# A reordered opening, input powers in two halves of the pairs, and half of the power turns ahead of the inner matrices, in a two-layer hybrid encoder

## The chip, the cores and the metric

The kernel runs on 1 core of one Trainium2 chip. The metric is the device time of one execution in microseconds (us); the median over runs is quoted. PE is TensorE, DVE is VectorE, ACT is ScalarE, POOL is GpSimd, SP is SyncE (here only a DMA queue).

## The reference, cut to what matters

Two pre-norm layers over 256 tokens of 1024 channels, and a final norm. A layer normalizes, projects with `w_in` (1024 x 4096) to q, k, v, the input u of a state-space mixer and four blocks of gate logits, and merges differential attention and the mixer:

```
xn = rms_norm(x, norm_mix[layer]); proj = xn @ w_in[layer]
q, k = rotary(q), rotary(k);  a = diff_attention(q, k, v, lam)
# s5_bidirectional, per direction, 32 groups, 64 complex states:
b_bar = ((a_bar - 1.0) / lam)[..., None] * b_mat
states = associative_scan(a_bar, einsum(b_bar, u));  y = y + real(einsum(c_mat, states))
s = gelu(y); s = s * sigmoid(s @ w_glu)
x = x + (gates0 * (a @ w_branch0) + gates1 * (s @ w_branch1)) @ w_out
x = x + (swiglu in layer 0, top-2-of-8 expert swiglu in layer 1)
```

## The kernel before, in words

Every engine has its own program, written out by hand, and semaphores order them. A weight tile is 128 x 2048 float32 (1 MB) in one of 3 (later 11) `raw` buffers. Each product is made of three: ACT copies the tile to a rounded `hi`, DVE subtracts to get `lo`, and PE multiplies hi by hi, lo by hi and hi by lo, 24 matmuls of 512 columns for a tile. `split_static(t)` is ACT's and DVE's share of tile t, `split_half(t, half)` the same in two halves, `proj` PE's. SP loads tile t once `lo` of tile t-3 is made. Two tiles are one block of 512 output columns: tiles 0 and 1 are u, 2 and 3 v, 4 and 5 q, 6 and 7 k (into the PSUM banks `PJ`), and tiles 8 to 15 (gates) are spread over the eight steps of the score loop.

The mixer works in chunks of four tokens, so it needs powers of the state factor times the input matrix. In layer 0 DVE makes them: `next_factor(k)` makes the small factors, `input_power(whole(bbar), 0)` the matrix itself, `input_power(b_power(k), k)` the powers 1 to 4, each over all 16 pairs of groups: four operations of 512 elements a partition, then two subtractions and two additions that lay the result out. In layer 1 POOL makes them long ahead. PE then transposes the powers in eight turns (`b` turns, one for each two pairs; ACT copies each to SBUF; the turns alternate between the two banks `TR`), and multiplies the small inner matrices of the chunks (`inner(l)`: 256 matmuls of 64 columns and 16 with the diagonal `kdiag`). `b_part` and `b_ready` tell PE that the powers are made.

After the inner matrices ACT copies them in two parts (`inner_copies`), and 16 DMAs of SP (`inner_moves`, `cbm_in`) lay them out; the first use is `y_inner` in step 0 of the score loop, right behind tile 8. Step s of that loop: PE scores(s), transposed weights, one weight tile, inner outputs, `s5_out(s)`; DVE `row_max`, `lo` of a tile, `softmax_factors`, `rotated(s+1)`, `weights(s)`, `scanned(s+1)`; POOL turns the scanned states back (`turn_forward`), for which `s5_out` waits.

PE's order around the change is: tiles 0 to 3, u transposes, tiles 4 to 7, q transposes, `inner`, k transposes, eight b turns with the first state matmuls between them, scores. POOL makes the parameters (`par_ready`) from two sines of ACT.

## Time and profile before

| what | value |
|---|---|
| runs of the kernel before | 1391.1, 1395.47, 1395.57 us; median 1395.47 |
| the profiled execution | 1390.18 us, of which the span is 1388.4 us |
| PE busy | 1350.3 us, 97% |
| DVE busy | 1107.1 us, 80% |
| ACT busy | 897.8 us, 65% |
| POOL busy | 332.5 us, 24% |
| chain that ended last | PE 86%, DVE 6%, ACT 3% |

The chain is the work followed back from the last instruction. A busy PE is counted from modelled ends. Times in the rows are from the start of the span, so the 1.8 us between the time and the span lie outside of them.

### The profile page before, as it was taken

How to read it: one execution, taken by the hardware profiler on the slowest of the kernel's cores; microseconds unless marked ns; L12 is line 12 of the kernel's file. 1: busy time of each engine (PE TensorE's matmuls, PEld its weight loads, DVE VectorE, ACT ScalarE, POOL GpSimd, SP SyncE). 2: the span in 40 equal slices, each digit the busy share in tenths (PEclk: the TensorE clock that was granted, in tenths of full speed). 3: DMA queues.
4: the chain of work that ended last, by engine and by line, in shares of the span. 5: the costliest groups of instructions: out<-in, count | busy, mean ns of one | idle time of the engine just before them, and what ended most of it. 6: DMA issues, size and time to landing. Idle time of an engine off the chain costs nothing.

```text
span 1388.4 us, 22394 instructions
## 1 busy us (share of the span) xinstructions
PE 1350.3 (97%) x7982; PEld 1108.9 (80%) x7982; DVE 1107.1 (80%) x1013; ACT 897.8 (65%) x915; POOL 332.5 (24%) x425
## 2 busy tenths in 40 slices
PE   8889999999999999999999999999999999999996
PEld 6678787888888787878888888888888888888885
DVE  6988678555565686788888889888888888898886
ACT  6366745444454566457777777777777777777775
POOL 7958419994000384010000000000000000000100
PEclk9999999999999999999999999999999999999998
DMA  8342355655645432979999999999999999999991
GB/s 330 122 127 104 137 171 193 197 182 186 198 145 173 132 123 99 351 264 339 369 374 377 386 366 377 391 362 387 379 375 388 368 375 390 352 391 350 386 347 31
DMA packets 194574, 385.12 MB, mean 277 GB/s; under 512 B 17616, under 2 KB 56912, under 8 KB 194384
## 3 DMA queue, kind: packets, MB, share of 16 engines
q1 hardware_dynamic: 189392, 369.99, 74.0%
q0 software_dynamic: 3360, 12.06, 2.9%
q10 hardware_dynamic: 1760, 2.23, 0.5%
q8 instruction: 39, 0.64, 0.2%
q14 instruction: 23, 0.19, 0.0%
HBM read 375.85 MB, written 7.34 MB: 276 GB/s over the span
## 4 chain that ended last, share of the span: by engine, by line
PE 86%; DVE 6%; ACT 3%; issue 2%; DMA 1%; SPq 1%; POOL 1%; ACTq 0%; POOLq 0%; DVEq 0%
PE bank L698 80%; DVE lo L1747 3%; ACT hi L1303 1%; PE bank L1197 1%; PE bank L716 1%; PE bank L842 1%; DMA raw<-in_w_in_dram 1%; PE bank L867 1%; PE bank L954 0%; PE bank L1180 0%; POOL raw L2346 0%; PE bank L1071 0%; ACT raw L1353 0%; ACT at_hi L1654 0%; PE bank L824 0%
## 5 line engine op out<-in xcount | busy, mean ns | idle before, releaser
L1747 DVE TENSOR_TENSOR lo<-raw,hi 128x2048 fp32r<-128x2048 f32 x344 | 801.7, 2342 | 153.7 <-ACT hi L1303 153.0
L1303 ACT ACTIVATE hi<-raw 128x2048 fp32r<-128x2048 f32 x344 | 658.0, 1916 | 186.3 <-PE bank L698 183.6
L698 PE MATMUL bank<-hi,at_hi 128*128 128x512 f32 x1288 | 513.5, 399 | 14.3 <-DVE lo L1747 3.4
L698 PE MATMUL bank<-hi,at_lo 128*128 128x512 f32 x1288 | 503.6, 391 | 0.0
L698 PE MATMUL bank<-lo,at_hi 128*128 128x512 f32 x1288 | 502.8, 391 | 0.1
L698 PEld LDWEIGHTS bank<-hi,at_hi 128*128 128x128 f32 x1288 | 242.7, 188 | 68.6 <-issue 7.6
L698 PEld LDWEIGHTS bank<-hi,at_lo 128*128 128x128 f32 x1288 | 242.5, 188 | 52.3
L698 PEld LDWEIGHTS bank<-lo,at_hi 128*128 128x128 f32 x1288 | 242.8, 189 | 47.9 <-DVE lo L1762 0.5
L698 PE MATMUL bank<-hi,ht_hi 128*128 128x512 f32 x432 | 168.8, 391 | 0.9 <-DVE ht_lo L2212 0.9
L698 PE MATMUL bank<-hi,ht_lo 128*128 128x512 f32 x432 | 168.2, 389 | 0.0
L698 PE MATMUL bank<-lo,ht_hi 128*128 128x512 f32 x432 | 168.1, 389 | 0.0
L2435 POOL TENSOR_TENSOR small<-cst 128x1 f32<-128x1 f32 x14 | 5.9, 422 | 591.0 <-DVE slot_row L2249 298.7
L698 PEld LDWEIGHTS bank<-hi,ht_hi 128*128 128x128 f32 x432 | 81.1, 188 | 19.2 <-DVE lo L1747 1.5
L698 PEld LDWEIGHTS bank<-hi,ht_lo 128*128 128x128 f32 x432 | 81.1, 188 | 17.0
L698 PEld LDWEIGHTS bank<-lo,ht_hi 128*128 128x128 f32 x432 | 81.2, 188 | 16.6
L1663 ACT ACTIVATE ht_hi<-bank 128x512 fp32r<-128x512 f32 (+1 forms) x48 | 26.9, 561 | 55.8 <-PE bank L1197 55.8
L1659 ACT ACTIVATE vreg<-bank 128x512 f32<-128x512 f32 (+1 forms) x48 | 27.1, 565 | 25.1 <-PE bank L698 25.1
L2341 POOL MEMSET raw<- 128x4 f32 x4 | 0.3, 105 | 156.4 <-DVE raw L1850 156.4
L1327 ACT ACTIVATE at_hi<-bank 128x512 fp32r<-128x512 f32 x28 | 15.4, 596 | 32.6 <-PE bank L716 32.6
L2212 DVE TENSOR_TENSOR ht_lo<-bank,ht_hi 128x512 fp32r<-128x512 f32 (+1 forms) x48 | 30.7, 640 | 1.7 <-ACT ht_hi L1663 1.7
L1608 ACT ACTIVATE ht_hi<-bank 128x512 fp32r<-128x512 f32 x10 | 6.0, 599 | 38.9 <-PE bank L1071 38.9
L2208 DVE TENSOR_TENSOR vreg<-vreg,bank 128x512 f32<-128x512 f32 (+1 forms) x48 | 30.5, 636 | 0.0
(312 smaller groups left out, 1172.5 us busy)
## 6 DMA issues: line engine op xcount, KB each, us to landing
raw<-in_moe_w_dram SPq DMA_DIRECT2D x528, 512.0 KB, 6.7
raw<-in_ffn_w_dram SPq DMA_DIRECT2D x66, 512.0 KB, 4.4
raw<-in_w_in_dram SPq DMA_DIRECT2D x64, 512.0 KB, 4.6
raw<-in_w_branch_dram SPq DMA_DIRECT2D x16, 512.0 KB, 4.4
raw<-in_w_out_dram SPq DMA_DIRECT2D x16, 512.0 KB, 4.8
raw<-in_w_glu_dram SPq DMA_DIRECT2D x4, 512.0 KB, 4.3
moe_sum<-xres POOLq DMA_DIRECT2D x3, 512.0 KB, 6.0
qk<-in_x_cols_dram SPq DMA_DIRECT2D x2, 512.0 KB, 6.2
```

The source lines that it names most:

```text
L698: return pe.matmul(o, a, b, start=start, stop=stop)
L716: last = pe.transpose(bank[:, i * rows:(i + 1) * rows], src, ident[0:rows, 0:rows])
L842: last = pe.matmul(o[rows, :], cblk[rows, r, q, 4 * d:4 * d + 4, :].rearrange("p i h -> p (i h)"), states, start=False, stop=m % 4 == 3 an ...
L867: m = pe.matmul(bank[r0:r0 + GC, c0:c0 + 64], bbar[rows, r, q, d, :], cblk[rows, r, q, 4 * d:4 * d + 4, :].rearrange("p i h -> p (i h)"), ...
L1197: m = pe.transpose(TR[0][:, f * P:(f + 1) * P], v_flat[:, f * P:(f + 1) * P], ident)
L1303: act.activation(hi[:, slot, :], src, ACT.Copy).then_inc(hi_ready, 1)
L1327: act.activation(at_hi[:, k0:k0 + kn, c0:c0 + P], bank[:, 0:kn * P].rearrange("p (k c) -> p k c", k=kn), ACT.Copy, scale=scale).then_inc(a ...
L1659: act.activation(v_flat[:, 0:h_width(c)], PJ[0][:, 0:h_width(c)], ACT.Silu).then_inc(g_ready, 1)
L1663: act.activation(ht_rows_hi[:, 0:h_width(c) // P, :], TR[0][:, 0:h_width(c)].rearrange("p (f s) -> p f s", s=P), ACT.Copy).then_inc(ht_hi_ ...
L1747: tt(lo[:, slot, :], src, hi[:, slot, :].bitcast(f32), SUB).then_inc(lo_ready, 1)
L2208: tt(v_flat[:, 0:h_width(c)], v_flat[:, 0:h_width(c)], right, MUL).then_inc(h_done, 1)
L2212: tt(ht_rows_lo[:, 0:h_width(c) // P, :], TR[0][:, 0:h_width(c)].rearrange("p (f s) -> p f s", s=P), ht_rows_hi[:, 0:h_width(c) // P, :].b ...
```

## The change

It does nine things. (1) x's second half of columns is loaded ahead of the token rows `xres`, and the loads of constants and parameters are spread behind tiles 3 to 6; (2) all of tiles 0 to 3 are split and multiplied in halves, and v (tiles 2, 3) goes to the banks `TR`; (3) ACT makes six of x's eight gained parts (before, four) and DVE two, and ACT's sines and squares stand behind the halves of tiles 1 and 2; (4) tiles 4 and 5 (q) go ahead of the u transposes on PE; (5) DVE makes the input powers in two halves of the pairs, pairs 8 to 15 of all powers first, after q's rotation; (6) the b turns 6, 7, 4, 5 go ahead of `inner` and the k turns, in both layers; (7) the diagonal `kdiag` is loaded ready-made; (8) the attention lambdas are summed after k's rotation; (9) in the score loop DVE does `rotated`, `softmax_factors`, `scanned`, `weights`, and `lo` last.

```diff
-B_TURNS = (6, 7, 0, 1, 2, 3, 4, 5)
+B_EARLY, B_LATE = (6, 7, 4, 5), (0, 1, 2, 3)
...
                         if t == 1:
-                            sp.dma_start(xres[:, :, :].rearrange("p t d -> p (t d)"), x_rows).then_inc(x_in, 16)
                             sp.dma_start(x_flat[:, 1024:2048], x_cols[:, 1024:2048]).then_inc(cols_second, 16)
                         if t == 3:
-                            sp.dma_start(cst[:, C_ID:C_ID + P], consts[:, C_ID:C_ID + P]).then_inc(ident_in, 16)
+                            sp.dma_start(xres[:, :, :].rearrange("p t d -> p (t d)"), x_rows).then_inc(x_in, 16)
+                        if t == 4:
                             sp.dma_start(braw_flat, ssm_b[0, :, :]).then_inc(b_in[0], 16)
+                        if t == 5:
...
                 pe.wait_ge(rot_ready, 4 * l + 2)
                 for th in range(TH):
                     transposes((l, "q", th), heads_of(qk[:, 0, :, :], th))
-                inner(l)
-                pe.wait_ge(rot_ready, 4 * l + 4)
-                for th in range(TH):
-                    transposes((l, "k", th), heads_of(qk[:, 1, :, :], th))
-                pe.wait_ge(b_ready, l + 1)
-                for g in B_TURNS:
+                pe.wait_ge(b_early, l + 1)
+                for g in B_EARLY:
+                    power_turn(g)
+                inner(l)
+                pe.wait_ge(rot_ready, 4 * l + 4)
+                for th in range(TH):
+                    transposes((l, "k", th), heads_of(qk[:, 1, :, :], th))
+                pe.wait_ge(b_ready, l + 1)
+                for g in B_LATE:
+                    power_turn(g)
...
+                    x_hi((0, 1))
+                    split_half(0, 0)
+                    split_half(0, 1)
                     act.wait_ge(lr_ready, 1)
                     act.activation(row(R_er), row(R_lr), ACT.Exp)
+                    act.wait_ge(cols_second, 16)
+                    x_hi(range(4, KD))
+                    split_half(1, 0)
+                    split_half(1, 1)
                     act.wait_ge(angle_ready, 1)
                     act.activation(par[:, SIN, :], row(R_red), ACT.Sin)
...
-            def input_power(dst, k):
+            def input_power(dst, k, first=0, end=PAIRS):
...
+                    rotary(l, "q", qk[:, 0, :, :])
+                    split_static(t + 7)
+                    dve.wait_ge(states_first, 2)
+                    for k in range(1, 5):
+                        input_power(b_power_end(k), k, 8, PAIRS)
+                    dve.memset(early_mark, 0.0).then_inc(b_early, 1)
+                    for k in range(1, 5):
+                        input_power(b_power_start(k), k, 0, 8)
+                    dve.memset(dve_mark, 0.0).then_inc(b_part, 1)
+                    dve.memset(power_mark, 0.0).then_inc(b_ready, 1)
+                    rotary(l, "k", qk[:, 1, :, :])
...
-                    if s in LOOP_PROJ[l] and s < 7:
-                        split_static(loop_proj(l, s)[0] + 2)
+                    if s < 7:
+                        rotated(l, s + 1)
                     softmax_factors(l, s)
                     if s < 7:
-                        rotated(l, s + 1)
+                        scanned(l, s + 1)
                     weights(l, s)
                     if s < 7:
-                        scanned(l, s + 1)
+                        split_static(loop_proj(l, s)[0] + 2)
```

PE, layer 0, from the last q transposes (the first two rows). Before, the inner matrices come next (`L858` with the diagonal, `L867` the 64 x 16 ones; a count stands for a run of equal rows), then the k transposes, and the b turns behind them:

```order
L716 MATMUL bank<-cst,qk 128x128 [waits tr_free1]
L716 MATMUL bank<-cst,qk 128x128 x3
L858 MATMUL bank<-raw,cst 16x4x16 [waits kdiag_ready,c_ready,b_part,loads]
L858 MATMUL bank<-raw,cst 16x4x16 x3
L867 MATMUL bank<-raw 16x64 x64
L858 MATMUL bank<-raw,cst 16x4x16 x4
L867 MATMUL bank<-raw 16x64 x64
L716 MATMUL bank<-cst,qk 128x128 [waits tr_free0,rot_ready]
L716 MATMUL bank<-cst,qk 128x128 x3
```

Now, in the same place:

```order
L729 MATMUL bank<-cst,qk 128x128 [waits tr_free1]
L729 MATMUL bank<-cst,qk 128x128 x3
L968 MATMUL bank<-cst,raw 128x128 [waits tr_free0,b_early]
L968 MATMUL bank<-cst,raw 128x128 x3
L968 MATMUL bank<-cst,raw 128x128 [waits tr_free1]
L968 MATMUL bank<-cst,raw 128x128 x3
L968 MATMUL bank<-cst,gates 128x128 [waits tr_free0]
L968 MATMUL bank<-cst,gates 128x128 x3
L968 MATMUL bank<-cst,gates 128x128 [waits tr_free1]
L968 MATMUL bank<-cst,gates 128x128 x3
L872 MATMUL bank<-raw,cst 16x4x16 [waits kdiag_in0,c_ready,b_part,loads]
```

Four b turns of four transposes each have moved ahead of the inner matrices, each waiting for ACT's copy of the turn two before it.

DVE, layer 0, the making of one power. Before, one whole power stands between the `lo` of two tiles:

```order
L1873 TENSOR_TENSOR raw<-bank,raw 128x512 [waits states_first]
L1873 TENSOR_TENSOR raw<-bank,raw 128x512
L1875 TENSOR_TENSOR bank<-bank,raw 128x512 x2
L1878 TENSOR_TENSOR gates<-raw,bank 128x12x2x16 [waits dve_own]
L1879 TENSOR_TENSOR gates<-raw,bank 128x12x2x16
L1878 TENSOR_TENSOR raw<-raw,bank 128x4x2x16
L1879 TENSOR_TENSOR raw<-raw,bank 128x4x2x16
L1747 TENSOR_TENSOR lo<-raw,hi 128x2048 [waits hi_ready,dve_own]
```

Now all powers stand behind q's rotation and the `lo` of tile 7; the end half of power 1 (pairs 8 to 15) is the first:

```order
L1775 TENSOR_TENSOR lo<-raw,hi 128x2048 [waits hi_ready]
L1904 TENSOR_TENSOR raw<-bank,raw 128x256 [waits states_first]
L1904 TENSOR_TENSOR raw<-bank,raw 128x256
L1906 TENSOR_TENSOR bank<-bank,raw 128x256 x2
L1909 TENSOR_TENSOR gates<-raw,bank 128x4x2x16 [waits dve_own]
L1910 TENSOR_TENSOR gates<-raw,bank 128x4x2x16
L1909 TENSOR_TENSOR raw<-raw,bank 128x4x2x16
L1910 TENSOR_TENSOR raw<-raw,bank 128x4x2x16
```

A power of 8 operations has become one of 8 and one of 6 (the start half has one destination), of half the elements, and the tiles' `lo` no longer wait between powers.

## Rows read from the trace of the kernel before

**Rows 1.** Busy time by stretch: PE, PEld, DVE, ACT, POOL, PEclk, DMA share, GB/s

```profile
40.00:50.00 10.00, 10.00 (x39) 8.09 (x38) 9.86 (x17) 1.92 (x1) 9.84 (x8) 0.86 0.60 204
...
800.00:1000.00 200.00, 199.57 (x911) 164.17 (x910) 177.70 (x118) 149.46 (x107) 6.87 (x8) 1.00 1.03 377
```

**Rows 2.** Timeline of PE, layer 0: start, us, line, form, count [idle before]

```profile
39.23 0.63 PE L698 MATMUL bank<-hi,at_hi 128*128 128x512 f32 x1 [3.37 <-DVE lo L1747]
...
46.40 0.39 PE L698 MATMUL bank<-hi,at_hi 128*128 128x512 f32 x1
...
68.98 0.30 PE L858 MATMUL bank<-raw,cst 16*16 16x64 f32 x8 [0.20 <-DVE raw L1886]
...
78.12 1.06 PE L954 MATMUL bank<-cst,raw 128*128 128x128 f32 x8 [0.34 <-ACT qk L1590]
79.44 1.14 PE L954 MATMUL bank<-cst,gates 128*128 128x128 f32 x8 [0.25 <-ACT raw L1353]
...
86.05 0.67 PE L698 MATMUL bank<-qk,ureg 128*128 128x256 f32 x2 [0.79 <-ACT raw L1353]
...
92.55 0.45 PE L824 MATMUL bank<-raw 64*64 64x64 f32 x8
```

**Rows 3.** Timeline of DVE, layer 0, from the factors to k's rotation

```profile
27.66 0.38 DVE L1858 TENSOR_TENSOR raw<-par 128x64 f32<-128x64 f32 x1
...
35.51 0.61 DVE L1954 TENSOR_TENSOR gates<-gates 128x256 f32<-128x256 f32 x1
...
39.10 1.28 DVE L1873 TENSOR_TENSOR raw<-bank,raw 128x512 f32<-128x512 f32 x2
...
41.62 0.56 DVE L1878 TENSOR_TENSOR gates<-raw,bank 128x384 f32<-128x384 f32 x1
...
42.55 0.28 DVE L1878 TENSOR_TENSOR raw<-raw,bank 128x128 f32<-128x128 f32 x1
...
43.06 2.80 DVE L1747 TENSOR_TENSOR lo<-raw,hi 128x2048 fp32r<-128x2048 f32 x1
...
67.95 0.06 DVE L1970 MEMSET small<- 128x1 f32 x1
...
73.63 2.29 DVE L1747 TENSOR_TENSOR lo<-raw,hi 128x2048 fp32r<-128x2048 f32 x1
```

**Rows 4.** Timelines of DVE, ACT and POOL, the first 23 us

```profile
11.23 1.33 DVE L2088 TENSOR_SCALAR at_hi<-qk,gates 128x256 fp32r<-128x256 f32 x4 [0.90 <-DMA qk<-in_x_cols_dram]
...
6.74 1.99 ACT L1322 ACTIVATE hi<-raw 128x1024 fp32r<-128x1024 f32 x2
8.75 1.28 ACT L1454 ACT_TABLE_LOAD   x1
...
12.68 0.43 POOL L2371 TENSOR_TENSOR gates<-gates 128x64 f32<-128x64 f32 x1 [0.52 <-ACT gates L1455]
...
22.22 0.29 POOL L2386 TENSOR_TENSOR par<-par 128x64 f32<-128x64 f32 x1
```

**Rows 5.** Timeline of SP, and line 599's time from issue to landing

```profile
77.39 11.97 SPq L599 DMA_DIRECT2D raw<-areg  x16
...
DMA to landing us min/median/max: 2.0/2.0/3.0
```

**Rows 6.** Timelines of POOL and PE, step 7 of each layer's score loop

```profile
152.28 1.29 POOL L2345 TENSOR_TENSOR raw<-raw 128x512 f32<-128x512 f32 x1 [3.41 <-DVE raw L1850]
...
156.36 1.15 PE L842 MATMUL bank<-raw 64*64 64x64 f32 x32 [1.21 <-POOL raw L2353]
...
540.40 1.15 PE L842 MATMUL bank<-raw 64*64 64x64 f32 x32 [0.90 <-POOL raw L2353]
```

**Rows 7.** Timelines of PE and ACT, layer 1, from the inner matrices to the scores

```profile
456.36 0.30 PE L858 MATMUL bank<-raw,cst 16*16 16x64 f32 x8
...
471.28 0.67 PE L698 MATMUL bank<-qk,ureg 128*128 128x256 f32 x2 [0.79 <-ACT raw L1353]
...
457.75 0.70 ACT L1583 ACTIVATE q_second<-bank,cst 128x512 f32<-128x512 f32 x1
```

264 lines of the change are left out of this document (134 added, 130 removed).

## The prediction, as it was put on record

> **What bounds the kernel now.** I read the busy time by stretch first. In the expert stage PE is busy 199.57 of 200 us [rows 1], so behind the opening PE sets the time, and what makes the score loop start earlier is kept to the end; what PE loses anywhere is lost. The opening is different. Its timeline of PE has waits of over 3 us for DVE's `lo` (3.37 us ahead of 39.23 [rows 2]), and DVE is busy 9.86 of 10 us there [rows 1]. DVE's timeline [rows 3] shows why: from the factors at 27.66 to the mark behind the last power at 67.95 it has a chain of 40.3 us with hardly a hole, in which the `lo` of tiles stand between powers of 4 us each (39.10 to 43.06). PE starts the inner matrices 1.0 us behind that mark, at 68.98, held up by DVE's diagonal for the last 0.20 us [rows 2]. So the layer-0 opening is DVE's until 68.98; then come PE and ACT in turns (inner matrices, k, b turns) up to the scores at 86.05, and PE reaches the first inner outputs at 92.55 [rows 2]. Those need the 16 DMAs, issued from 77.39 to 89.36 and landing 2.0 us after an issue [rows 5].
>
> **Tiles 0 to 7 (halves, x ahead of the token rows, v in other banks, q ahead of u's transposes).** All of PE's waits for `lo` up to tile 7 may go. A matmul takes 199.57 / 911 = 0.22 us [rows 1], a tile of 24 some 5.3 us; from 9.1 on (DVE has tile 0's halves at 10.3, 0.90 ahead of 11.23 [rows 4], the first one 1.2 earlier) eight tiles and about 2 us of u transposes end near 54, where before the inner matrices began at 68.98 [rows 2], behind 1 us of q transposes. PE could be there some 13 us earlier. I count this at nothing by itself, since PE then waits for the powers: DVE is what hides it. If DVE's chain were shorter, it would be worth up to those 13 us.
>
> **When DVE's chain starts.** Its factors need POOL's parameters, which before were ready at 22.5, unused until 27.66 [rows 3, 4]. Now nothing stands ahead of them but tile 3's halves. POOL's second part starts with ACT's sines (12.68 [rows 4]), and these move behind x's second half and the halves of tile 1: the columns landed at 11.2 [rows 4] with 1 MB of token rows ahead of them, which at some 400 GB/s are 2.6 us (an estimate), so at 8.6 now; then four gained parts (as on DVE, 1.33 [rows 4]), two halves (1.99), a table load (1.28) and the sines (about 0.4) [rows 4]. That is 13.7 against 12.6: 1.1 us late. Parameters at 23.6, the chain starts 4.1 us earlier.
>
> **What is in the chain.** The lambda sums leave it (the first of two operations takes 0.61 [rows 3], some 1.1 together). The halving adds work. Four 512-element operations with the wait behind them take 2.52 us (39.10 to 41.62), so 0.60 each; two of 384 take 0.93, 0.47 each; one of 128 lasts 0.28 against 0.56 for 384 [rows 3]. A straight line through 0.60 and 0.47 gives 0.33 for 256 and 0.20 for 128, that is 0.07 us for an operation whatever its size. A power goes from 8 operations to 14, and the matrix itself from 6 to 12: 30 operations more, 2.0 us; and each half waits for its own writes twice, about 0.1 us each, ten times more: 1.0 us. The mark moves to 23.6 + 40.3 + 3.0 - 1.1 = 65.8. The bounds: 0 for the 30 operations at best, twice 2.0 at worst.
>
> The Trainium skill (VectorE: DVE Perf Modes, section The TRN2 errata) gives 120 cycles at 0.96 GHz, 125 ns, as an operation's fixed share when it reads PSUM. By that the 30 operations cost 3.8 us and not 2.0, and the gain below would be 1.8 us less. The rows show starts nearer to each other than that, and the sum goes by the rows.
>
> **From the mark to the scores.** The diagonal is loaded now, so the inner matrices start at about 65.9 instead of 68.98: 3.1 us gained. k's rotation follows the mark by 5.7 us less the diagonal's 0.7 (67.95 to 73.63 [rows 3]), done at 70.8, ahead of the inner matrices' end (some 73.7), as before. Behind them two turns less (6, 7) stand ahead of turn 0: 78.12 to 79.44, 1.3 us; turns 4 and 5 go too, another 1.3 us and about 0.4 of the 0.79 us that PE waits for ACT's last copy [rows 2]. That makes 3.0 us, if the four early turns are free. In layer 0 they are: PE is idle from about 55 on, they need only the end halves (about 57), and end near 60. Scores at 79.9, and PE ready for the inner outputs at 86.4.
>
> **A new wait.** The 16 DMAs hang on ACT's copy of the inner matrices, not on the b turns. They move by 3.1 us only: the last, issued at about 88.7 before, lands at 87.6 now. PE, in order, waits 1.2 us there with the state matmuls and all of step 1 behind it. Gain at this point 92.55 - 87.6 = **4.9 us**.
>
> **The clock.** PE is idle for about 5.9 us ahead of 65.9. Behind the idle 3.37 us ahead of 39.23 its matmuls took 0.63 instead of 0.39, and the granted clock was 0.86 of full in that stretch [rows 1, 2], the level of 1.2 GHz for a part of it. The inner matmuls would meet this. Whether a run of 64-column matmuls suffers, no row shows; 0 if the instruction stream paces them, at most doubled for the 1.9 us of the first bank. I take **0.4 us lost**.
>
> **Layer 1.** There POOL's powers are long ready and PE has no hole. The early turns start behind ACT's four q copies, which end at 458.45 [rows 7]; turn 6 gets in earlier (its bank is free), and 7, 4, 5 follow at 0.66 each (half of 1.32). So the inner matrices start at about 460.4 instead of 456.36: 4.0 us. Behind them the same 3.0 us are saved (the 0.79 wait is there too [rows 7]). **1.0 us lost**. The DMAs move by 4.0 and would land just ahead of PE.
>
> **The score loop.** In step 6 `rotated` and `scanned` stand behind a `lo` of some 3 us, and so POOL starts only at 152.28, and PE waits for it 1.21 us in layer 0 and 0.90 us in layer 1 [rows 6]. With `lo` last POOL starts some 3 us earlier, and both waits go: **1.2 and 0.9 us gained**. `lo` is needed two steps later, which hides its move. The scaling of `subln`, now behind the loop, fits into DVE's hole there.
>
> **The sum.** 4.9 - 0.4 - 1.0 + 1.2 + 0.9 = 5.6 us. The profiled execution took 1390.18, so 1384.6 for one like it. The runs of before had a median of 1395.47; 1395.47 - 5.6 = **1389.9 us**, 0.40%.
>
> **Rivals.**
> 1. *The forecast*: 4 to 7.5 us gained, 1388 to 1391.5. Chance 0.55.
> 2. *More*: the 30 operations and the ten waits cost nothing, since DVE overlaps them (the pair at 39.10 is marked 1.28 us, more than two steps of 0.60 [rows 3]). Then the mark, the inner matrices and the DMAs move by 3.0 us more: 8.6 us gained, 1386.9. Against it: the line through 128, 384 and 512 elements. Chance 0.10.
> 3. *No measurable change*: DVE's chain gives nothing back. If the parameters come 1 us later still, the operations cost twice 2.0 us and layer 1 pays 0.5 more, 5.6 - 3.5 = 2.1 us are left: 1393.4. For it: DVE's own work grows; the 13 us at PE are hidden behind it either way. Chance 0.28.
> 4. *Slower, by the clock*: after its idle stretch PE stays at 1.2 GHz through the inner matrices, the turns and tile 8. The price is worked out from 0.63 against 0.39 us (start to start about 0.43 against 0.23): tile 8 costs 4.8 more, the inner matmuls up to 3.8. From 5.6 us on it decides; in full it is 8.6, with the time at 1398.5. Against it: before, the clock came back within some 4 us of work. Chance 0.07.
>
> The skill (TensorE: Matmul & The Clock Gate, Part 1) has the half rate as the default state, which activity releases, and warns of idle gaps between bursts; the row at 39.23 agrees. It speaks for the fourth rival, since the change leaves PE one long gap where there were three short ones.
>
> **How the numbers follow.** 0.3% is 4.2 us, about what a measurement of this kernel can tell from no change. The forecast lies 1.4 us above that and a part of it (gains from 4 to 4.2, and the scatter of a median) falls below: faster 0.55 + 0.10 - 0.02 = 0.63, same 0.28 + 0.02 = 0.30, slower 0.07. The range leaves out the fourth rival and the far ends of the second: 1384 to 1394.5. The likeliest case's own is 1388 to 1391.5.
>
> **What would show it.** PE: tiles 1 to 7 without a wait over 0.5 us, then idle for 5 to 6 us ahead of L881; that line starts at 65 to 67. DVE: the memset of `b_part` at 65 to 67, and starts 0.33 us apart for 256 elements. POOL's last parameter at 23 to 24.5. Scores at 79 to 81 and 1.2 us of waiting for SP's DMAs ahead of the first inner outputs (L838). In layer 1 the inner matrices 4 us behind the q transposes. No wait for POOL in step 7. The prediction is wrong if the sines are much later, if the halves of an operation take more than 0.4 us each, or if the clock stays low past the inner matrices.

## The result, and the profile after

The changed kernel takes 1384.03 us (median of 5 runs, 1383.31 to 1384.47); the kernel before took 1392.04 us (5 runs, 1390.62 to 1395.57). The medians stand 8.0 us (0.58%) apart. The ratio, taken over all runs, is 0.9935, 95% interval 0.9917 to 0.9953: faster, clear of noise. The forecast was 1389.9. The profiled execution took 1384.23, with a span of 1382.4; that of before took 1390.18 with 1388.4, so the profiled pair stands 6.0 us apart.

TensorE of the changed kernel in layer 0, to be read against [rows 2]: start, us, line, form, count, and in brackets the idle time and what ended it (L881, L872 and L838 are the lines 867, 858 and 824 of before).

```profile
56.98 1.81 PE L968 MATMUL bank<-cst,raw 128*128 128x128 f32 x8 [1.92 <-DVE small L1989]
...
66.01 0.41 PE L872 MATMUL bank<-raw,cst 16*16 16x64 f32 x8 [5.41 <-DVE small L1992]
66.35 3.61 PE L881 MATMUL bank<-raw 64*16 64x64 f32 x128
...
70.23 2.24 PE L881 MATMUL bank<-raw 64*16 64x64 f32 x128
72.40 1.10 PE L729 MATMUL bank<-cst,qk 128*128 128x128 f32 x8
...
79.21 0.67 PE L711 MATMUL bank<-qk,ureg 128*128 128x256 f32 x2 [0.60 <-ACT raw L1377]
...
87.14 0.45 PE L838 MATMUL bank<-raw 64*64 64x64 f32 x8 [1.34 <-DMA raw<-areg]
```

PE waits 1.92 us for the end halves ahead of the early turns (56.98), which costs nothing since it waits for the powers behind them anyway; then comes one idle stretch of 5.41 us up to the inner matrices at 66.01 (68.98 before). The last row is the first inner output: 87.14 instead of 92.55, so 5.41 us are gained here, and PE waits 1.34 us for the DMAs (`raw<-areg`, SP's 16 copies). The 128 matmuls of the first bank last 3.61 us. The windows of the same kernel say why (columns as in [rows 1]: PE, PEld, DVE, ACT, POOL, PEclk, DMA share, GB/s):

```profile
65.00:70.00 5.00, 3.99 (x144) 3.63 (x144) 4.74 (x13) 0.00 (x0) 4.63 (x13) 0.50 0.01 3
70.00:75.00 5.00, 4.56 (x152) 3.80 (x149) 4.96 (x4) 2.68 (x6) 4.92 (x5) 0.92 0.05 10
```

The granted clock is 0.50 while they run, which is 1.2 GHz, behind PE's idle stretch. From 70 to 75 it is 0.92. In the same place before, the inner matrices ran at a clock of 1.00, but with two holes, idle stretches that the profile names "issue" because nothing that it shows ended them:

```profile
72.73 0.29 PE L858 MATMUL bank<-raw,cst 16*16 16x64 f32 x6 [1.33 <-issue]
...
76.46 0.29 PE L867 MATMUL bank<-raw 64*16 64x64 f32 x6 [1.56 <-issue]
```

These holes are absent here, so the whole block of inner matrices took 6.4 us (66.01 to 72.40) instead of 7.7 (68.98 to 76.69) in spite of the low clock.

DVE, ACT and POOL, against [rows 3, 4]:

```profile
24.26 0.23 DVE L1888 TENSOR_TENSOR raw<-par 128x64 f32<-128x64 f32 x1 [1.07 <-POOL par L2415]
...
47.34 0.74 DVE L1904 TENSOR_TENSOR raw<-bank,raw 128x256 f32<-128x256 f32 x2
48.01 0.75 DVE L1906 TENSOR_TENSOR bank<-bank,raw 128x256 f32<-128x256 f32 x2
...
65.85 0.06 DVE L1992 MEMSET small<- 128x1 f32 x1
...
14.53 0.26 ACT L1485 ACTIVATE par<-gates 128x64 f32<-128x64 f32 x1 [0.57 <-POOL gates L2397]
```

POOL's last parameter is ready at 24.2, DVE's factors start at 24.26, and the mark behind the last power stands at 65.85. The chain took 41.6 us. Pairs of 256-element operations start 0.67 us apart (47.34, 48.01), so 0.33 each; those of 128 elements start 0.20 apart (48.79 and 48.99 in the same timeline).

SP's queue, against [rows 5]:

```profile
73.11 12.43 SPq L607 DMA_DIRECT2D raw<-areg  x16
```

The score loop, against [rows 6]: POOL starts step 6 at 142.31 instead of 152.28, and PE waits for POOL in step 7 of neither layer.

```profile
142.31 1.29 POOL L2374 TENSOR_TENSOR raw<-raw 128x512 f32<-128x512 f32 x1 [3.51 <-DVE raw L1880]
...
148.78 1.15 PE L856 MATMUL bank<-raw 64*64 64x64 f32 x32
...
534.73 1.15 PE L856 MATMUL bank<-raw 64*64 64x64 f32 x32
```

Layer 1, against [rows 7]:

```profile
447.88 1.03 PE L729 MATMUL bank<-cst,qk 128*128 128x128 f32 x8
449.93 0.63 PE L968 MATMUL bank<-cst,raw 128*128 128x128 f32 x4 [1.01 <-ACT q_second L1611]
...
452.93 0.30 PE L872 MATMUL bank<-raw,cst 16*16 16x64 f32 x8
...
455.92 0.22 PE L872 MATMUL bank<-raw,cst 16*16 16x64 f32 x1 [0.56 <-issue]
...
459.37 0.23 PE L881 MATMUL bank<-raw 64*16 64x64 f32 x1 [1.33 <-issue]
...
466.54 0.67 PE L711 MATMUL bank<-qk,ureg 128*128 128x256 f32 x2 [0.69 <-ACT raw L1377]
```

The inner matrices start at 452.93 (456.36 before), 5.05 us behind the q transposes at 447.88, and they hold two holes named issue, of 0.56 and 1.33 us.

### The profile page after: what moved, and what is told of

It reads as the page before. It is cut to its first block, busy times and chain, and to the rows that moved or that the text cites. A ratio compares the mean times of both kernels' runs of the same rounds, so it can differ in the third digit from the quotient of the medians.

```text
span 1382.4 us, 22446 instructions
## 1 busy us (share of the span) xinstructions
PE 1349.6 (98%) x7982; PEld 1109.7 (80%) x7982; DVE 1104.4 (80%) x1041; ACT 899.4 (65%) x918; POOL 339.7 (25%) x427
## 4 chain that ended last, share of the span: by engine, by line
PE 88%; DVE 4%; ACT 2%; issue 2%; POOL 1%; SPq 1%; DMA 0%; ACTq 0%; DVEq 0%; POOLq 0%
PE bank L711 83%; DVE lo L1775 2%; PE bank L1221 1%; PE bank L856 1%; ACT hi L1327 1%; PE bank L729 1%; SPq L607 1%; PE bank L881 1%; DVE raw L1904 1%; DVE bank L1906 0%; PE bank L1204 0%; PE bank L1095 0%; PE bank L838 0%; ACT at_hi L1682 0%; DMA gates<-in_ssm_rows_dram 0%
## 5 line engine op out<-in xcount | busy, mean ns | idle before, releaser
L2375 POOL TENSOR_TENSOR raw<-raw 128x512 f32<-128x512 f32 x16 | 45.1, 2821 | 0.0
L473 POOL TENSOR_TENSOR raw<-raw,par 128x512 f32<-128x512 f32 (+2 forms) x24 | 31.3, 1326 | 0.6
```

The costliest lines, as they stand in the source:

```text
L473: tt(t1[:, r, q0:q1], source(r, q0, q1), num(re, q0, q1), MUL)
L2375: tt(po2, zs[:, ::-1, :], w[:, 1:2, :].broadcast_to([P, 2, 256]), MUL).then_inc(zs_used, 1)
```

## The experiments

The kernels were measured in five batches ("calls" in the expectations), each with the kernel before beside them on one chip. "Before" had medians of 1392.37, 1391.38, 1394.14, 1392.82 and 1391.34 us in the five batches (17, 11, 14, 11 and 11 runs). Its fastest runs differ by batch too (1390.65, 1389.21, 1390.31, 1392.30, 1389.75), so a difference within one batch is firmer than one across batches.

| kernel | median us | lowest to highest | batch |
|---|---|---|---|
| x1, the change again | 1384.72 | 1383.38 to 1385.45 | 1 |
| x2, before with the new loop order | 1388.56 | 1386.38 to 1394.08 | 1 |
| x3, change, layer 1's turns as before | 1381.20 | 1380.27 to 1382.23 | 1 |
| x4, change, whole powers, all turns late | 1381.60 | 1380.73 to 1381.88 | 1 |
| x5, x4 with the old loop order | 1384.71 | 1384.16 to 1385.19 | 2 |
| x6, change with fillers | 1381.35 | 1381.02 to 1381.61 | 2 |
| x7, change, half of the DMAs on POOL's queue | 1383.98 | 1383.07 to 1386.53 | 2 |
| x8, x4 with that queue | 1381.24 | 1380.55 to 1381.77 | 2 |
| x9, before with fillers | 1388.84 | 1387.94 to 1389.63 | 3 |
| x10, x3 with fillers and that queue | 1383.65 | 1381.61 to 1384.56 | 3 |
| x13, x3 with fillers | 1380.01 | 1379.64 to 1380.39 | 4 |
| x14, x4 with fillers behind the wait | 1387.54 | 1386.55 to 1387.98 | 4 |
| x15, the change, third time | 1384.77 | 1384.33 to 1387.74 | 4 |
| x16, x4 with fillers ahead of the wait | 1380.27 | 1379.74 to 1381.06 | 5 |
| x17, x13 again | 1379.95 | 1379.16 to 1381.38 | 5 |

### The parts of the change

**x1.** The changed kernel as it is, as the base of the first batch.

> The changed kernel once more, beside the kernel before on one chip. Theory A (the profiles tell all of it): spans of 1382.4 against 1388.4 us, so 6.0 us less, and the 8.0 us between the medians shown is the scatter of the kernel before (1390.6 to 1395.6 in its runs). Rival B (something that the two profiled executions do not show): 8 us or more again in the medians.

1384.72, ratio 0.9932 (0.9914 to 0.9949): 7.7 us between the medians, nearer to the second reading, while the profiled execution (span 1383.6) stands 4.8 us below that of before.

**x2.** The kernel before, with only DVE's order in the score loop changed:

```diff
-                    if s in LOOP_PROJ[l] and s < 7:
-                        split_static(loop_proj(l, s)[0] + 2)
-                    softmax_factors(l, s)
                     if s < 7:
                         rotated(l, s + 1)
-                    weights(l, s)
+                    softmax_factors(l, s)
                     if s < 7:
                         scanned(l, s + 1)
+                    weights(l, s)
+                    if s < 7:
+                        split_static(loop_proj(l, s)[0] + 2)
```

> The kernel before with the new order of DVE in the score loop alone (rotated, softmax factors, scanned, weights, lo last). Theory A: PE's waits for POOL in step 7 of both layers go (1.2 and 0.9 us), and the late step 1 of layer 0 too (0.7 us, a step of 10.1 instead of 9.4 us): 2.9 us less than before. Rival C (the waits move on to the next one, ACT's or the channel matmuls): under 1 us.

1388.56, 3.8 us below before in its batch, where 2.9 were expected; the profiled span is 1385.2, 3.2 below that of before. The order is worth 3.2 us of the profiled pair, where the forecast had 2.1. The runs scatter as widely as those of before.

**x3.** The changed kernel, with the eight b turns of layer 1 behind k's again:

```diff
-B_EARLY, B_LATE = (6, 7, 4, 5), (0, 1, 2, 3)
+B_EARLY, B_LATE = ((6, 7, 4, 5), ()), ((0, 1, 2, 3), (6, 7, 0, 1, 2, 3, 4, 5))
```

> The changed kernel, with layer 1's eight b turns behind the k turns again. Theory A: the early turns cost layer 1 4.1 us ahead of the inner matrices and give back 1.3: 2.8 us less than the changed kernel, of which about 1.1 us is luck of the holes inside the inner matrices (1.9 against 0.9 us), so 1.7 to 2.8 us. Rival D (the early turns are free in layer 1, the loss is all in those holes): 1 us less at most.

1381.20, 3.5 us below x1, more than expected. TensorE of x3 in layer 1:

```profile
447.20 1.03 PE L729 MATMUL bank<-cst,qk 128*128 128x128 f32 x8
448.17 0.30 PE L872 MATMUL bank<-raw,cst 16*16 16x64 f32 x8
...
463.39 0.67 PE L711 MATMUL bank<-qk,ureg 128*128 128x256 f32 x2 [0.79 <-ACT raw L1377]
```

From the q transposes to the scores x3 takes 16.19 us (447.20 to 463.39), the changed kernel 18.66 (447.88 to 466.54): the early turns lose 2.5 us here (3.0 against x1, which has 19.20). They put the inner matrices 5.05 us behind the q transposes instead of 0.97; of the 2.5 us 0.6 are a difference in holes (1.25 us in x3, 1.89 in the changed kernel). The rest of the 3.5 lies ahead of this place: the two profiles reach the q transposes 0.68 us apart (x1 1.4), with the same code up to there.

**x4.** The changed kernel with whole powers and all b turns behind k's in both layers. What is left of the change is the reordered opening and the loop order:

```diff
-B_EARLY, B_LATE = (6, 7, 4, 5), (0, 1, 2, 3)
+B_EARLY, B_LATE = ((), ()), ((6, 7, 0, 1, 2, 3, 4, 5), (6, 7, 0, 1, 2, 3, 4, 5))
...
-                    input_power([(0, 8, [bbar[:, r, 0:8] for r in range(2)])], 0, 0, 8)
+                    input_power(whole(bbar), 0)
...
-                    input_power([(8, PAIRS, [bbar[:, r, 8:PAIRS] for r in range(2)])], 0, 8, PAIRS)
...
-                        input_power(b_power_end(k), k, 8, PAIRS)
+                        input_power(b_power(k), k)
...
-                    for k in range(1, 5):
-                        input_power(b_power_start(k), k, 0, 8)
```

> The changed kernel with whole input powers and all eight b turns behind the k turns, in both layers; what is left is the reordered opening and the loop order. Theory A: DVE's chain sets layer 0 and is 3.1 us shorter (30 operations and ten waits less), so the mark of the powers at 62.8 instead of 65.9; the four turns cost 3.0 behind the inner matrices; scores at about 79 as before, but the 16 DMAs start 3 us earlier, so their wait of 1.3 us goes; with layer 1's 2.8: 4 to 5 us less than the changed kernel, 1379 to 1380. Rival E (the two halves and the early turns carry the gain of the opening): slower than the changed kernel by 1 to 3 us.

1381.60, 3.1 us below x1, where 4 to 5 were expected. DVE and TensorE of x4:

```profile
63.35 0.06 DVE L1988 MEMSET small<- 128x1 f32 x1
...
63.65 0.41 PE L872 MATMUL bank<-raw,cst 16*16 16x64 f32 x8 [7.76 <-DVE small L1988]
...
80.68 0.67 PE L711 MATMUL bank<-qk,ureg 128*128 128x256 f32 x2 [0.78 <-ACT raw L1377]
...
87.20 0.45 PE L838 MATMUL bank<-raw 64*64 64x64 f32 x8
```

DVE's mark stands at 63.35, 2.5 us earlier than in the changed kernel: this is the price of the halves (3.0 in the forecast). The scores come at 80.68, 1.5 us later, since all turns stand ahead of them, and the first inner outputs at 87.20, against 87.14: the changed kernel reaches the scores earlier and gives it back in the wait for the DMAs. So the halves and the early turns together bring nothing in layer 0; x4 and x3, which differ in nothing else, are 0.4 us apart.

**x5.** x4 with DVE's old order in the loop (the diff of x2, reversed).

> The kernel with whole powers and all b turns behind k's (1381.6), with the old order of DVE's work in the score loop put back, so that only the reordered opening is left of the change. Theory A (the parts add up; the loop order is worth the 3.2 us that two profiles stood apart): 1384 to 1385.5, and since the reordered opening is in it, the runs stay within 3 us of each other. Rival (the runs of before that lie 3 to 5 us above its fastest are due to the loop order): the runs scatter over 5 us or more, and the median is 1385 or above. Rival B (the opening alone gives the 4.9 us of the forecast's opening term plus the 1 to 2.8 us that layer 1 lost): 1385 to 1387. In the profile PE waits for POOL in step 7 in both layers again (1.2 and 0.9 us before).

1384.71, as expected, and PE waits for POOL in step 7 again (1.22 us in layer 0). The order of the loop is worth 3.1 us here too (across two batches; 3.5 against x8, which is x4 with another queue, in the same batch). The runs lie within 1.0 us: the narrowness is the opening's, not the loop's.

### The clock, and why the kernel before scatters

**x6.** The changed kernel with matmuls that compute nothing that is used, in layer 0 while PE waits for the powers (they came out as 128x512, 0.24 us each, not 128x256 as the expectation says):

```diff
+                if l == 0:
+                    filler((l, "b", B_EARLY[0]), 4)
                 pe.wait_ge(b_early, l + 1)
                 for g in B_EARLY:
                     power_turn(g)
+                if l == 0:
+                    filler((l, "k", 0), 20)
                 inner(l)
```

> The changed kernel with 24 matmuls more (128x256) that compute nothing that is used, in layer 0 while PE waits for DVE's powers: 4 ahead of the early turns and 20 behind them, up to about 63 us. Theory A (the inner matrices ran 1.7 us longer in their first bank since the granted clock was 0.50 there, and this cost is real): the clock is above 0.8 at the inner matrices, L881's first bank takes under 2.5 us and the time falls by 1 to 1.7 us, to 1382.5 to 1383.5. Rival (the instruction stream sets the pace of these 64-column matmuls; at the full clock the holes of 1.3 and 1.6 us that the kernel before had come back): the first bank is short, but holes named issue of about 2.9 us stand in L881 and the time moves by less than 0.7 us. Rival B (the filler makes the turn buffers or ACT late): slower by over 1 us.

1381.35, some 3 us below the changed kernel (1384.03, 1384.72, 1384.77 in its three draws): more than the 1 to 1.7 expected. The changed kernel did not run in this batch; beside x6 stands x7, the change with another queue, with 1383.98, 2.6 us above it, and the profiled executions of x6 and of the changed kernel are 2.9 us apart. TensorE of x6:

```profile
65.95 0.30 PE L872 MATMUL bank<-raw,cst 16*16 16x64 f32 x8 [1.49 <-issue]
66.18 1.98 PE L881 MATMUL bank<-raw 64*16 64x64 f32 x128
...
70.66 0.86 PE L881 MATMUL bank<-raw 64*16 64x64 f32 x48 [1.04 <-issue]
...
85.34 0.45 PE L838 MATMUL bank<-raw 64*64 64x64 f32 x8 [0.51 <-DMA raw<-areg]
```

At a granted clock of 1.00 the first bank takes 1.98 us and not 3.61. A hole of 1.04 us named issue stands in the second. k's transposes start at 71.45 instead of 72.40, and PE meets the DMAs with 0.51 us of waiting. In x1 such a hole came beside the low clock:

```profile
73.52 0.53 PE L881 MATMUL bank<-raw 64*16 64x64 f32 x24 [1.32 <-issue]
```

So both readings hold in part: the low clock costs 1.7 us in the first bank and its diagonal (66.01 to 69.89 is 3.88 us, against 2.14 in x6), and holes come and go; x6 was spared most of both, in layer 1 too (one hole of 0.79 us, against 1.89 in the changed kernel and 2.43 in x1).

**x9.** The kernel before with fillers in its three holes of over 3 us: 13 ahead of tile 1, 10 ahead of tile 4, 13 ahead of tile 6.

```diff
                 for i in range(2, 8 - len(LOOP_PROJ[l]) // 2):
+                    if l == 0:
+                        bank = open_turn((l, "q", 0))
+                        for _ in range(10 if i == 2 else 13):
+                            mm(bank[:, :], at_hi[:, 0, 0:P], at_hi[:, 0:2, :], True, True)
                     proj(t + 2 * i, l, i, 0, True, False)
...
                 for t, half in ((0, 1), (1, 0), (1, 1)):
+                    if (t, half) == (1, 0):
+                        for _ in range(13):
+                            mm(TR[0][:, :], at_hi[:, 0, 0:P], at_hi[:, 0:2, :], True, True)
```

> The kernel before with 36 matmuls more (128x256) that compute nothing that is used, in its three holes of over 3 us: 13 ahead of tile 1, 10 ahead of tile 4, 13 ahead of tile 6. Theory A (the runs of before at 1395 to 1397, whose mean granted clock is 0.992 to 0.993 against 0.993 to 0.997 of the others, are executions in which the clock fell once more, or for longer, after one of these holes): with the holes filled the mean clock is 0.997 or more in every run, no run lies over 3 us above the fastest, and the median is 1389 to 1391, since DVE sets the opening and the matmuls at half the clock between 40 and 60 us cost nothing there. Rival (the scatter comes from elsewhere, such as DMA or the expert stage): runs at 1395 to 1397 remain in about one of four. Rival B (the fillers delay tile 4 or 6 at PE and so DVE's reading of q and k): 1 to 2 us slower than the fast runs of before.

1388.84, with nine runs from 1387.94 to 1389.63 (mean granted clock 0.997 or 0.998 in eight of them, 0.995 in the slowest), where the 14 runs of before in the same batch reached from 1390.31 to 1398.24. The windows of x9 and its inner matrices:

```profile
15.00:20.00 5.00, 4.27 (x20) 3.20 (x19) 3.61 (x5) 4.98 (x6) 4.53 (x9) 1.00 1.05 389
40.00:45.00 5.00, 5.00 (x24) 4.14 (x23) 4.93 (x8) 0.00 (x0) 4.92 (x5) 1.00 0.63 210
...
69.08 0.30 PE L861 MATMUL bank<-raw,cst 16*16 16x64 f32 x8 [1.80 <-DVE raw L1893]
```

The clock is 1.00 at 40 to 45 us (0.71 before), and the inner matrices start at 69.08, as before at 68.98: DVE sets this. What the fillers remove is the spread: seven of the 14 runs of before lie at 1394.7 or above, and none of the nine of x9. The median falls by 5.3 us, but not all of it is the spread: the profiled execution of x9 is 1.8 us below that of before, and has these 1.8 in the inner matrices, which ran without a hole (69.08 to 74.87, before 68.98 to 76.69). Of the 64 runs of before in the five batches 43 lie at 1393.52 or below and 21 at 1394.76 or above, and the means of their times follow the mean granted clock, with overlap between neighbouring rows (at 0.993 the runs go from 1390.72 to 1396.93):

| mean clock | runs of before | mean us |
|---|---|---|
| 0.991 | 6 | 1396.9 |
| 0.992 | 9 | 1396.0 |
| 0.993 | 13 | 1394.4 |
| 0.994 | 16 | 1392.2 |
| 0.995 | 11 | 1391.2 |
| 0.996 and 0.997 | 9 | 1390.8 |

**x11 and x12.** The kernel before, unchanged, for two more profiles.

> The kernel before, unchanged, for one more profile. With a chance of about one in four the profiled execution is one of those at 1395 to 1397. Theory A of the scatter (the granted clock): in such a profile the added 4 to 5 us lie in stretches with the clock below 1 in which PE sets the time. Rival: they lie in DMA or in DVE's chain at the full clock.

> As the profile a of the kernel before: a second draw, with the same readings by either theory.

Neither was one of the upper group: 1392.58 and 1390.42. But x11 shows a way from the clock to the time. One window and two rows of the first profile of before:

```profile
15.00:20.00 5.00, 2.69 (x12) 2.24 (x13) 3.94 (x5) 4.98 (x5) 4.69 (x7) 1.00 1.05 389
...
21.78 0.69 ACT L1366 ACTIVATE ureg<-bank,small 128x512 f32<-128x512 f32 x1 [1.52 <-PE bank L698]
...
31.66 1.29 DVE L1873 TENSOR_TENSOR raw<-bank,par 128x512 f32<-128x512 f32 x2
```

And x11: the same window, ACT's first copy of u, DVE's `lo` of tile 3, one of its last factors and the start of the matrix itself (`input_power` for k = 0), POOL beside them, and TensorE's tile 4 and inner matrices:

```profile
15.00:20.00 5.00, 2.52 (x7) 2.03 (x8) 3.88 (x5) 4.94 (x6) 4.61 (x8) 0.80 1.06 392
...
23.57 0.69 ACT L1366 ACTIVATE ureg<-bank,small 128x512 f32<-128x512 f32 x1 [3.10 <-PE bank L698]
...
26.53 2.54 DVE L1762 TENSOR_TENSOR lo<-raw,hi 128x1024 fp32r<-128x1024 f32 x2 [4.84 <-ACT hi L1322]
...
32.49 1.08 DVE L1859 TENSOR_TENSOR raw<-raw,par 128x64 f32<-128x64 f32 x1
...
35.61 1.29 DVE L1873 TENSOR_TENSOR raw<-bank,par 128x512 f32<-128x512 f32 x2
...
32.34 2.16 POOL L465 TENSOR_TENSOR raw<-raw,par 128x512 f32<-128x512 f32 x2
...
43.68 0.79 PE L698 MATMUL bank<-hi,at_hi 128*128 128x512 f32 x1 [6.03 <-DVE lo L1747]
...
72.19 0.30 PE L858 MATMUL bank<-raw,cst 16*16 16x64 f32 x8 [1.12 <-DVE raw L1886]
```

The clock fell behind the hole of 3.44 us ahead of tile 1, and was 0.80 and 0.86 from 15 to 25 us, where the first profile of before has 1.00 (and so has x12, although its hole there is 3.63 us). Here TensorE is what others wait for: ACT's copy of u comes at 23.57 instead of 21.78, `lo` of tile 3 at 26.53 instead of 25.16, and DVE's factors start at 29.00 instead of 27.66, 1.3 us late. A further 2.6 us arise in these factors themselves: the matrix itself starts at 35.61 instead of 31.66. Being late, the last three factor operations met POOL's operations of 512 elements (from 32.34 on), and took 1.08, 0.95 and 1.09 us, where they had taken 0.35, 0.21 and 0.18 and had ended before POOL reached its own at 32.74. That this meeting is what slowed them is read from the two traces and was not tried. So the low clock is the start of the delay and the smaller part of it. In the end tile 4 starts at 43.68 instead of 39.23 and the inner matrices at 72.19 instead of 68.98, and the execution ended 2.4 us later.

The Trainium skill (TensorE: Matmul & The Clock Gate, Part 1) says that the number of matmuls that one kernel runs at the low clock varies from run to run. The three profiles of before agree: from 15 to 25 us x11 has the low clock, the other two have not. TensorE of the changed kernel has no wait between 10 and 54 us, and its granted clock is 1.00 over that whole stretch.

### The DMAs of the inner matrices

**x7.** The changed kernel with 8 of the 16 DMAs issued by POOL:

```diff
-                for e in range(2):
+                for e in range(1):
...
+                    if m == 0:
+                        pool.wait_ge(kc_ready, 2 * (l + 1))
+                        for g in range(2):
+                            for i in range(4):
+                                r0, s0 = 64 + GC * i, 64 * g + 32
+                                pool.dma_start(cbm[r0:r0 + GC, :, g, :],
+                                               kc[s0:s0 + GC, :, GC * (3 - i):GC * (3 - i) + 64]).then_inc(cbm_pool[l], 16)
```

> The changed kernel with 8 of the 16 DMAs of the inner matrices issued by POOL instead of SP, in both layers. Theory A (SP issues them one after the other in 12.4 us, and the last one's landing costs PE the 1.34 us ahead of the first inner outputs): SP's part takes about 6.2 us, the wait at L838 goes, and the time falls by 1.0 to 1.4 us, to 1382.7 to 1383.1. Rival (POOL takes longer to issue one than SP's 0.78 us, and its own work for the scores and tables is put back): the wait stays or moves to POOL's work in step 1 or 2 and the time is the same or up to 4 us longer. Rival B (SP's issues of weight tiles stand behind the 16, and come 6 us earlier now): DMA queues fuller near 75 to 85 us, with no effect on PE.

1383.98, 0.05 to 0.8 us below the three draws of the changed kernel, all in other batches: the expected 1.0 to 1.4 us are not there in the median, and a smaller gain is not settled. The profiled execution was the fastest of the six (1383.07; the slowest took 1386.53). It shows the wait gone, and the first inner outputs 1.34 us earlier:

```profile
77.39 4.46 POOL L2449 DMA_DIRECT2D raw<-areg  x8
...
85.80 0.45 PE L840 MATMUL bank<-raw 64*64 64x64 f32 x8
```

**x8.** x4 with the same edit.

> The kernel with whole powers and all b turns behind k's (1381.6) with the 8 DMAs on POOL's queue. Its PE had no wait for these DMAs, since the scores and all eight turns stand between. Theory A: no change, within 1 us of 1381.6. Rival (the change of queues costs POOL's time): 1383 or more, and by the same amount the result of the kernel with the early turns is masked, so that the difference between the two tells what the DMA wait alone was worth.

1381.24 against x4's 1381.60 in another batch: no change, as expected.

**x10.** x3 with the fillers and POOL's queue.

> The changed kernel with layer 1's turns as before, the 24 filler matmuls in layer 0, and half of the 16 DMAs on POOL's queue. Theory A (the three effects add up: 3.1 us for layer 1, 3.0 for the clock, 0.4 to 1.3 for the DMA wait): 1377.3 to 1378.2. Rival (the filler's gain contains a part of the others', since a shorter run of inner matrices only moves PE to a later wait): 1379 to 1380.5.

1383.65: 2.3 us slower than x6 alone, and 3.6 slower than x13 below, which differs from it only in the queue. Both readings had a gain and both missed. TensorE, and the DMAs by queue (KB each, median us from issue to landing):

```profile
87.86 0.69 PE L840 MATMUL bank<-raw 64*64 64x64 f32 x8 [3.16 <-DMA raw<-areg]
...
raw<-areg SPq DMA_DIRECT2D x8, 32.0 KB, 2.1
raw<-areg POOLq DMA_DIRECT2D x8, 32.0 KB, 5.1
```

POOL's eight DMAs take 5.1 us to land, and PE waits 3.16 us for them. Behind this wait TensorE's clock is down as well (0.70 from 85 to 90 us, 0.62 from 90 to 95). SP issued weight tiles from 78.84 on, since its own part was shorter, and POOL's DMAs of 77.31 to 81.77 met them; in x7, with the weight tiles from 80.00 on, POOL's landed in 2.9 us. That the weight tiles delayed them fits both traces and was not tried by itself.

### What adds up

**x13 and x17.** x3 with the fillers of x6, in two batches.

> The changed kernel with layer 1's turns as before and the 24 filler matmuls in layer 0, all 16 DMAs on SP's queue. Theory A (3.1 us for layer 1 and about 3.0 for the clock are independent, and what spoilt the kernel with all three edits at 1383.65 is POOL's queue): 1377.8 to 1378.8. Rival (the two overlap: the clock's gain is partly given back where PE meets the DMAs of the inner matrices earlier): 1379 to 1380.5. In the profile the inner matrices run at a granted clock of 1.00 and PE waits less than 1 us for the DMAs.

> The changed kernel with layer 1's turns as before and the 24 fillers, once more, as the base of the run beside it: 1379.6 to 1380.4, as the first time.

1380.01 and 1379.95: the fastest kernel. x13 is 0.9903 (0.9889 to 0.9916) of before in its batch and 4.8 us below x15 beside it. Together the two edits bring 4.8, alone 3.5 and about 3.2 (the latter across batches): they share some 2 us, and the rival's time was right. Its reason fits only in part: PE waits 0.60 us for the DMAs in x13 and not at all in x17. In layer 1 x6 had one hole of 0.79 us where the changed kernel has two, and x13 has one of 1.16, so a part of what x3 took back was no longer there to take.

**x15.** The changed kernel in the batch of x13.

> The changed kernel once more, on the chip of this call, as the base of the other two. By the two earlier draws (1384.03, 1384.72) its median is 1383.8 to 1385.0, its runs within 2.5 us, and the kernel before in the same call has runs both at 1390 to 1393 and at 1395 to 1398, since its holes of over 3 us stand in work that sets the time. Rival (the width of before belongs to a chip or to a call): before's runs here stay within 3 us.

1384.77, as expected, but with one run at 1387.74, which no profile explains: the changed kernel is steadier than before, not wholly steady. Before had four of 11 runs at 1395.6 or above. The profile of x15 has the clock down in layer 1, behind the second hole of the inner matrices (1.60 us):

```profile
460.00:465.00 5.00, 4.62 (x59) 3.75 (x58) 0.00 (x0) 3.65 (x9) 0.00 (x0) 0.66 0.23 43
```

**x14.** x4 with 24 fillers. They stood behind the wait for `b_early`, which the whole powers signal only with the last mark, so they ran after it.

> The kernel with whole powers and all b turns behind k's (1381.6), with 24 filler matmuls ahead of the inner matrices of layer 0. Theory A (halves and early turns bring nothing in layer 0, at either clock): within 1 us of the kernel with layer 1's turns as before and fillers. Rival (at the full clock the early turns are worth more, since the turns behind the inner matrices are then what PE lacks time for; or less, since the DMAs' landing comes to limit): over 1 us apart, with the sign telling which.

1387.54, 5.9 us slower than x4, and no answer to its question:

```profile
63.56 8.41 PE L711 MATMUL bank<-at_hi 128*128 128x512 f32 x24 [7.58 <-DVE small L1992]
```

It measures something else. The 24 fillers take 8.41 us, 0.35 each, since they start at the low clock (0.50 from 60 to 65 us, 0.57 from 65 to 70) and end at the full one. All of it stands on the path; the inner matrices start 8.25 us later than in x4 (71.90), and 2.0 us come back, since they now run at the full clock (scores at 86.93 against 80.68).

**x16.** The same fillers ahead of the wait.

```diff
+                if l == 0:
+                    bank = open_turn((l, "k", 0))
+                    for _ in range(24):
+                        mm(bank[:, :], at_hi[:, 0, 0:P], at_hi[:, 0:2, :], True, True)
                 pe.wait_ge(b_early, l + 1)
```

> The kernel with whole powers and all b turns behind k's, with the 24 filler matmuls now ahead of PE's wait for the powers (in x14 they stood behind it and so ran 8.4 us late). Theory A (halves and early turns bring nothing in layer 0, at either clock): within 1 us of the kernel with layer 1's turns as before and fillers, run beside it. Rival (at the full clock one of the two arrangements is ahead): over 1 us apart. In the profile the fillers end by about 63.3, the inner matrices start near 63.7 at a granted clock of 1.00.

1380.27, 0.3 us from x17 beside it, as the first reading had it: with the clock kept up the halves and early turns of layer 0 bring nothing either. The 24 fillers run in 5.75 us from 56.87 on, ahead of the wait, and the inner matrices start as early as in x4 (63.65):

```profile
63.70 0.30 PE L872 MATMUL bank<-raw,cst 16*16 16x64 f32 x8 [1.08 <-DVE small L1992]
```

## Why the prediction had the direction right and the size wrong

The forecast said faster by 5.6 us, 1389.9; the medians stand 8.0 apart, at 1384.03, 5.9 us below the forecast: on the lower edge of the range (1384 to 1394.5) and outside the likeliest case's own (1388 to 1391.5). The gain of 8.0 us is near that of the second rival (8.6), whose mechanism did not occur.

**The step that failed** is in two places.

The first is the base: "The runs of before had a median of 1395.47; 1395.47 - 5.6". Of the 5.9 us 3.4 are this base: with five runs the median of before is 1392.04. The text took the gain from one execution and the base from the median of three, two of which belonged to the upper group that holds 21 of 64 runs. The sum against the profiled execution itself gave 1384.6, and the profiled execution after took 1384.23.

The second is a term put at nothing, that of tiles 0 to 7: "I count this at nothing by itself, since PE then waits for the powers: DVE is what hides it". DVE hides the waits of TensorE in the profiled execution, but not in all of them. Behind a hole the clock can fall, and then TensorE is late for ACT and DVE: in x11 this put the inner matrices 3.2 us back. The change removes the holes, so its gain is larger, by up to 5 us, over the executions of the upper group: 8.0 us between the medians against 6.0 between the two profiled ones. [rows 2] showed the holes. That idle TensorE is behind the upper group is shown by x9, where matmuls that compute nothing took it away (none of nine runs, against seven of 14 beside them), and that the reordered opening does the same is shown by x5 (six runs within 1.0 us). The table of clocks agrees, but alone it could not tell cause from effect, since a longer wait also lowers the mean clock. That the upper group's 4 to 5 us arise as x11's 2.4 do is argued, since no profile caught such a run.

Step by step, on the profiled pair:

| term | forecast | measured |
|---|---|---|
| first inner outputs, layer 0 (4.9 - 0.4) | 4.5 | 5.4 |
| score loop, layer 0 | 1.2 | 2.2 |
| layer 1, q transposes to scores | -1.0 | -2.8 |
| score loop, layer 1 | 0.9 | 0.9 |
| sum | 5.6 | 5.7 (6.0 at the end) |

Each measured term is a difference of offsets between the two traces: 5.41 at the first inner outputs; 156.36 against 148.78 in step 7, so 7.58 there and 7.50 at the start of layer 1; 471.28 against 466.54 at the scores, 4.74; 540.40 against 534.73, 5.67.

That the two sums agree is luck: 0.9 and 1.0 us too little in layer 0 made up for 1.8 too little loss in layer 1. The first term also depends on the execution: the first inner outputs came 4.7 us earlier than before in x1 (87.82) and 6.1 in x15 (86.46).

- *DVE's chain.* Forecast 23.6, 65.8 and an inner start at 65.9; measured 24.2, 65.85 and 66.01. The sines came later than thought (14.53, where POOL's angles ended their wait), the halves were a little cheaper (2.5 against 3.0), and the errors met. The line through 128, 384 and 512 elements held: 0.33 for 256. The second rival, that the operations overlap, is out.
- *Tiles 0 to 7 free of waits*: right, and the 13 us hidden in the profiled execution too. What the waits cost in other executions was missed, as said above.
- *The clock.* Forecast 0.4 us lost. The first bank with its diagonal cost 1.7 us more (3.88 against 2.14), near the upper bound of 1.9; but the two holes of before (1.33 and 1.56 us) were absent in this profile, so the block took 6.4 us instead of 7.7, a gain that no term had. It is luck of the execution: in x1 a hole of 1.32 us came beside the low clock, and its block took 8.0. The fourth rival's condition came true for one bank, and the clock was back at 70 to 75: too short to decide.
- *The DMA wait.* Forecast 1.2, measured 1.34; it differs by execution (0.37 in x1, 0.16 in x15), with the time that SP took for its 16 issues (12.43 us, 11.53 in x1, 11.24 in x15) and with when the block ended. In x4 there is no wait.
- *Layer 1.* The start of the inner matrices is right to 0.1 (4.07 forecast as 4.0). Behind them only 2.46 us were saved instead of 3.0, and the block grew by 1.15, of which its holes are 0.99. The term was mis-sized by 1.8, and x3 against x1 puts it higher still, at 3.5.
- *The loop.* 3.1 against 2.1, x2 3.2 and x4 less x5 3.1. Besides the two waits of PE in step 7, step 1 of layer 0 took 9.37 us instead of 10.13. That too goes with DVE's order: x2, which has only the new order, has 9.36, and x5, which has the old one in the new kernel, 10.23.
- *Which part carries it.* The loop order 3.1 to 3.8, the reordered opening about 7 (x5, 6.7 below its before), layer 1's turns minus 2.5 to 3.5, halves with early turns in layer 0 nothing (0.3 to 0.4). The forecast gave the early turns 3.0 us behind the inner matrices of layer 0 and saw that the DMAs would take part of them back; that the halves' price in DVE's chain takes the rest was not put together.

## What to carry to other kernels

When a base spreads by more than the effect, take the gain and the base from the same execution, and look at the mean granted clock of each run before choosing a base. Idle stretches of TensorE that another engine hides can still cost, in some executions, in the work behind them. Two dozen matmuls that compute nothing, placed ahead of the wait, were worth about 3 us in the changed kernel; three dozen in the holes of before took away its upper group and 5.3 us of its median (1.8 of them, in the profiled pair, were holes in the inner matrices); two dozen behind the wait lost 6 us. Work moved ahead of a handoff pays only if nothing else lands last: in layer 0, under an idle TensorE, it reached the scores 1.5 us earlier and gave this back in a wait for DMAs; under a busy TensorE, in layer 1, the same edit cost 2.5 to 3.5 us.

## What the hardware showed beyond expectation

- 128 matmuls of 64x64 take 1.98 us at a granted clock of 1.00 and 3.61 at 0.50, so these small matmuls do follow the clock. The Trainium skill (TensorE: Matmul & The Clock Gate, Part 1) has activity release the half rate; x6 and x16 agree, whose matmuls that compute nothing keep the clock at 1.00 up to the inner matrices.
- In the blocks of 256 such matmuls holes of 0.56 to 1.60 us named issue stand in nearly every profile, at places that differ with the code (ahead of the last 48 matmuls of a bank in x6, the last 24 in x1, the last one in layer 1 of the changed kernel), and none stood in a bank that ran at the clock of 0.50. In x6, x13 and x17, which have the same code up to there, the hole of layer 0 stands ahead of the same 48 matmuls and lasts 1.04, 0.79 and 1.08 us. What they are was not tried.
- The clock fell in layer 1 of x15 (0.66 from 460 to 465) after a hole of 1.60 us only, in a stretch of small matmuls.
- DVE's small operations in SBUF slow down beside POOL's long ones in x11: 128x32 and 128x64 in 0.95 to 1.09 us, against 0.18 to 0.35 in the first profile of before, where POOL was at small operations then.
- A DMA issued by POOL took 0.56 us of its queue (4.46 for 8) against SP's 0.78 (12.43 for 16), and landed later: 2.9 us against SP's 2.2 in x7, and 5.1 against 2.1 in x10, with weight tiles in flight.
